# Expert weights by rows of sixteen kilobytes, a fourth split handed to GpSimd, and an earlier low half of the activations

## The chip, the core and the metric

The kernel runs on one core of one Trainium2 chip. The metric is the device time of one execution in microseconds. The kernel before takes 1289.53 us (median of three runs, 1288.2 to 1292.21). The execution that the profiler recorded took 1285.25 us; its span, from first to last instruction, is 1283.5 us.

## The reference

A decoder trunk with two residual layers on x of 512 tokens by 1024 features, float32. Each layer adds a mixer of the normed x (layer 0: gated recurrence beside differential attention; layer 1: gated linear attention), and then a mixture of experts:

```
h = rms_norm(x, ffn_norm)
per token: the best of 4 groups, the best 2 of its 4 experts, weights w
for e in 16 experts:
    act = silu(h @ w_gate[e]) * (h @ w_up[e])        # w_gate, w_up: 1024 x 512
    y  += combine[:, e] * (act @ w_down[e])          # w_down: 512 x 1024
x = x + y
```

A sum over the 1024 or 512 rows of a weight matrix may be taken in any order, if the rows of the weights and the columns of the other factor are ordered alike.

## The kernel before

Everything is written by engine, with semaphores written out by hand; no planner orders it. Float32 accuracy comes from splitting: a factor is rounded to a "high" part and the rest is the "low" part, and each product is three matmuls (high by high, high by low, low by high: `three`, L1106 to L1111).

Per layer, after the mixer, the second norm makes `h` (DVE, L1579), four tiles of 128 tokens. SyncE stores them as `h_rows` in DRAM. The router's scores are computed from x itself, DVE turns them into ranks and one-hots, and the first expert's rows are picked by matmul with a one-hot (L1343). Rows of the other experts are fetched by GpSimd with an indirect DMA of up to 96 rows (`gather`, L760 to L766), one expert at a time.

Then come the 16 experts, "blocks" 0 to 15 (`expert_loop`, L521; blocks 3 to 12 lie in a hardware loop of two blocks a turn). In block b:

- TensorE (`block_pe`, L1395): gate of expert b+1, with the four transposes of `act` of expert b in its middle (`act_T`, L1372, L1377); the eight transposes of the gathered rows of expert b+2 (`rows_T`, L1368); down of expert b; up of expert b+1. Gate, down and up are 24 matmuls of 512 columns each.
- ScalarE (`block_act`, L1028): the high part of the weights of down, in four pieces of 128x1024 (L870); the high part of `actT` (L1039); silu (L1024); the high part of up; the high part of the next rows (L1017); the high part of the next gate; the copy and store of y (L1060). Before each set of weights it waits until TensorE has finished the product before, since two sets share the buffers.
- VectorE (`block_ve`, L1872): the low part of the same weights, `low` (L1819, L1824: `expert_w - weight_high`, four pieces, each released by one piece of ScalarE's), for down, then the low part of `actT` (L1880), then `low` of up, the low part of the rows (L1832), `low` of gate, and `act = silu * up` (`times_up`, L1845). In block 1 it also computes slots (L1849), in block 13 the list of further blocks (`further`, L1858).
- SyncE (`block_loads`, L682) loads the next three weights of 2 MB (`load`, L649), each as soon as a product has freed its place. GpSimd only gathers (L801).

TensorE waits for a piece of low weights by a count on one semaphore (`wait_low`, L1357), and for the low part of `actT` before down (L1409, released by L1882). The last block's down weights ("LAST") are split apart from the others.

A weight matrix of 1024 rows lies in SBUF as 8 rows per partition; row k*128+p is in partition p. One partition's 8 rows (4 for down) are then 8 runs of 2 KB (4 of 4 KB) in DRAM.

Of the kernel before, what the change touches and what calls it, by code (L numbers as in the profile page):

```python
# [5 lines left out]
F32 = mybir.dt.float32  # L6
# [81 lines left out]
def build(nc, t):  # L88
# [149 lines left out]
    with ctx:  # L238
# [18 lines left out]
        def sem(name):  # L257
            return ctx.enter_context(nc.semaphore(name))
# [160 lines left out]
        oh0_ready = sem("first_onehot_ready")  # L419
        xgT_ready, ex_ready = sem("xgT_ready"), sem("gate_silu_ready")  # L420
        xgTh_ready, actTh_ready = sem("xgT_high_ready"), sem("actT_high_ready")
        w_hi, w_lo, w_lo_first = sem("weight_high_ready"), sem("weight_low_ready"), sem("first_low_ready")
        act_ready, actT_ready, y_ready, y_stored = sem("act_ready"), sem("actT_ready"), sem("y_ready"), sem("y_stored")
        yg_sem = [sem(f"y_gathered{i}") for i in range(2 * NT)]
# [128 lines left out]
        def high_count(l, pos, part):  # L553
            return SPLITS * (3 * NE * l + pos) + part + 1

        def low_count(l, pos, part):

            return SPLITS * ((3 * NE - 2) * l + pos - 2) + part + 1

        def parts(l, p0, par, part):  # L560

# [26 lines left out]
        def _(sp):  # L588
# [48 lines left out]
            for l in range(NL):  # L637
# [10 lines left out]

                def load(name, e, dst, done):  # L649

                    src = t["moe_w_" + name][l, bass.ds(e, 1)].rearrange("a (k p) n -> p (a k) n", p=P)
                    if name == "down":
                        dst = dst.rearrange("p (k c) n -> p k (c n)", c=2)
                    sp.dma_start(dst, src).then_inc(done, 16)
# [77 lines left out]
        def _(pool):  # L732
# [52 lines left out]
            for l in range(NL):  # L785
                for s in STEPS[l]:
                    if s == ("dT", 0, "dq", 0):
                        store_zeros()
                    if s[0] == "h":
                        power(xrs[:, s[2]:s[2] + 1])  # L790
                    elif s[0] == "sum":
                        power(dstd[:, s[3] % 2])
                    elif s[0] == "norm" or s[0] == "da" and s[2] >= 3 and (s[2] - 3) % NH == NH - 1:
                        power(rstd[:, 0:NH])

                pool.wait_ge(idx_ready, l + 1)
                pool.wait_ge(h_stored, 16 * NT * (l + 1))
                pool.sem_inc(gather_issued, 1)
                pool.indirect_dma_start(xg[0:CAP, :], None, hbuf[l][:], bass.IndirectOffsetOnAxis(idx[:, 1:2], 0)
                                        ).then_inc(gathered, 16)  # L800
                with pool.Fori(2, NE) as b:  # L801

                    bk.wait_full(pool, ("xgT", l), b - 1)
                    gather(l, b, idxcol_ready, b + (l * (NE - 2) - 1), gathered)
                pool.wait_ge(eid_ready, l + 1)
                more = pool.value_load(eid[0:1, 15:16], min_val=0, max_val=NX)
                pool.wait_ge(zero_stored, 16 * NL)
                with pool.If(more > 0):
                    pool.wait_ge(y_stored, 16 * (NE - 1) * (l + 1))
                    pool.wait_ge(ov_idx[l], 1)  # L810
                    with pool.Fori(0, NX) as b:
                        pool.wait_ge(ov_pe[l], b * 4 + 1)
                        gather(l, b + NE, ov_col[l], b + 1, ov_gathered[l])
                    pool.wait_ge(ov_act[l], 4 * NX)
                    gather_outputs(l, NB * CAP)
                with pool.If(more < 1):
                    pool.wait_ge(y_stored, 16 * (NE - 1) * (l + 1))
                    gather_outputs(l, NE * CAP)
# [283 lines left out]
        def _(pe):  # L1102
# [23 lines left out]
            for l in range(NL):  # L1126
# [230 lines left out]
                def wait_low(pos, b, part):  # L1357
                    if pos < 2:
                        pe.wait_ge(w_lo_first, SPLITS * (2 * l + pos) + part + 1)
                    else:  # L1360
                        pe.wait_ge(w_lo, b * (3 * SPLITS) + low_count(l, pos, part))

                def rows_T(b):
                    key = ("xgT", l)
# [107 lines left out]
        def _(ve):  # L1472
            link = Chain(ve, v_step)
            tt, ts, stt, cp = ve.tensor_tensor, ve.tensor_scalar, ve.scalar_tensor_tensor, ve.tensor_copy
            red = ve.tensor_reduce
            e_uses, n_st, roots = [0], [0], [0]

            def wait_e():
# [81 lines left out]
            for l in range(NL):  # L1560
# [7 lines left out]
                for s in STEPS[l]:  # L1568
                    kind = s[0]
                    if kind == "h":  # L1570
# [5 lines left out]
                                ve.wait_ge(h_stored, 16 * NT)  # L1576
                        ve.wait_ge(sq_done, NT * n + i + 1)
                        rsqrt(xrs[:, i:i + 1], xss[:, i:i + 1], D)
                        stt(h[:, i], x[:, i], xrs[:, i:i + 1], normw[:], ALU.mult, ALU.mult).then_inc(h_ready, 1)  # L1579
                    elif kind == "first" and s[2] == 0:  # L1580
                        first_low(0, range(SPLITS))
                        ve.wait_ge(rw_loaded, 16 * (NG + 4) * (l + 1))
# [254 lines left out]
                def times_up(b):  # L1837

                    ve.wait_ge(ex_ready, b + (l * NE + 1))

                    if l or not isinstance(b, int) or b:
                        s_, n_, _ = bk.uses[("actT", l)]
                        ve.wait_ge(bk.full[s_], b + (n_ - 1))
                    bk.wait_full(ve, ("up", l), b)
                    link(tt(act[0:CAP], bank(("up", l))[0:CAP], ex[0:CAP], ALU.mult))  # L1845
                    ve.sem_inc(act_ready, 1)
                    ve.sem_inc(bk.freed(("up", l)), 1)

# [23 lines left out]
                def block_ve(b, par):  # L1872

                    is_int = isinstance(b, int)
                    last = is_int and b == NE - 1
                    if not last:
                        low(DOWN, b, par)
                    key = ("actT", l)
                    ve.wait_ge(actTh_ready, b + (l * NE + 1))
                    link(tt(actTl[:].rearrange("p k n -> p (k n)"), bank(key)[:, 0:4 * CAP],  # L1880
                            actTh[:].rearrange("p k n -> p (k n)").bitcast(F32), ALU.subtract))
                    ve.sem_inc(actT_ready, 1)  # L1882
                    ve.sem_inc(bk.freed(key), 1)
                    if not last:
                        low(UP, b, par)
                    if not (is_int and b >= NE - 2):
                        rows_T(b + 2, par)
                        low(GATE + 3, b, par)
                    if is_int and b == NE - 2:
                        low(LAST, which=range(SPLITS - 1))  # L1890
                    if not last:
                        times_up(b + 1)
                    if is_int and b == NE - 2:
                        low(LAST, which=range(SPLITS - 1, SPLITS))
                    if is_int and b == 0:
                        slots()
                    if is_int and b == NE - 3:
                        further()
# [43 lines left out]
                with ve.If(more > 0):  # L1942
# [7 lines left out]
                    with ve.Fori(0, NX) as b:  # L1950
                        ve.wait_ge(ov_act[l], b * 4 + 2)
                        ve.wait_ge(ov_pe[l], b * 4 + 3)
                        tt(act[0:CAP], PS[0:CAP, 1, :], ex[0:CAP], ALU.mult).then_inc(ov_ve[l], 1)
            for kind, i in sums[NL - 1]:
                (add_gathered if kind == "x" else add_last)(NL - 1, i)

# [22 lines left out]
```

## Time and profile before

| | us |
|---|---|
| median of the runs | 1289.53 |
| the profiled execution | 1285.25 |
| its span | 1283.5 |
| TensorE busy | 1180.3 (92%) |
| VectorE busy | 914.7 (71%) |
| ScalarE busy | 674.1 (53%) |
| GpSimd busy | 97.3 (8%) |
| experts of layer 0, first to last matmul | about 361.6 to 661 |
| experts of layer 1 | about 966 to 1266 |

Busy times are of the profiled execution. A TensorE matmul is drawn with a length of 0.39 us although the next starts 0.23 us after it, so neighbours overlap, and short stops hide in the busy time; starts and named waits are the better reading. "PEld" is TensorE's weight load, "DVE" VectorE, "ACT" ScalarE, "POOL" GpSimd, "SP" SyncE. "DVEq L1882" as a releaser is the semaphore that VectorE's queue raises behind the instruction of L1880. Times of a timeline are counted from the span's start.

### The profile page before, as it was taken

The numbers are of one execution on the slowest core, as the hardware profiler recorded it, in microseconds if no ns is written. First come the engines' busy times: TensorE is split into PE (matmuls) and PEld (weight loads), VectorE is DVE, ScalarE is ACT, GpSimd is POOL, SyncE is SP. The second block draws the span as 40 slices with busy tenths as digits, with TensorE's granted clock in tenths as the row PEclk, the third lists the DMA queues.
The fourth block names the chain that finished last, engine by engine and source line by source line (L and its number), as shares of the span: only waits on it lengthen the run. The fifth ranks groups of instructions, "written<-read, shape, count | busy, mean of one in ns | idle before, by whom it ended". The sixth has DMA issues, their size and how long they took to land.

```text
span 1283.5 us, 16959 instructions
## 1 busy us (share of the span) xinstructions
PE 1180.3 (92%) x5788; PEld 898.5 (70%) x5788; DVE 914.7 (71%) x1251; ACT 674.1 (53%) x843; POOL 97.3 (8%) x128
## 2 busy tenths in 40 slices
PE   5999879999799999999878999999979999999986
PEld 4776669878776766766646688887876666667663
DVE  4646668656579888888967247646558898888886
ACT  4335651134347778777733242132426777787862
POOL 1120000000010000000030000001001100000003
PEclk9999999999899999999989999999979999999998
DMA  6231110123599999999860240113169999999955
GB/s 221 91 89 66 66 66 1 66 73 125 187 331 363 366 385 390 384 382 384 332 220 1 70 136 15 66 66 131 66 257 303 368 381 381 383 391 385 381 203 209
DMA packets 129423, 281.75 MB, mean 220 GB/s; under 512 B 18945, under 2 KB 19457, under 8 KB 129361
## 3 DMA queue, kind: packets, MB, share of 16 engines
q1 hardware_dynamic: 119680, 246.98, 53.2%
q0 software_dynamic: 5888, 20.97, 5.3%
q10 hardware_dynamic: 3792, 12.98, 2.7%
q8 instruction: 37, 0.61, 0.2%
q14 instruction: 26, 0.21, 0.1%
HBM read 262.05 MB, written 18.87 MB: 219 GB/s over the span
## 4 chain that ended last, share of the span: by engine, by line
PE 57%; DVE 25%; issue 9%; ACT 6%; POOL 1%; DMA 1%; DVEq 1%; ACTq 0%; SPq 0%
PE PS L1109 16%; PE PS L1111 15%; PE PS L1110 15%; DVE expert_w_low L1824 10%; PE PS L1213 4%; DVE group_low L1612 2%; PE PS L1343 2%; ACT weight_high L870 1%; PE PS L1148 1%; DVE xgT_low L1832 1%; DVE act L1845 1%; DVE score_max L1743 1%; DVE G L1502 1%; PE PS L1323 1%; DVE hT_low L1596 1%
## 5 line engine op out<-in xcount | busy, mean ns | idle before, releaser
L1824 DVE TENSOR_TENSOR expert_w_low<-expert_w,weight_high 128x1024 fp32r<-128x1024 f32 x368 | 426.5, 1221 | 75.0 <-ACT weight_high L870 71.3
L870 ACT ACTIVATE weight_high<-expert_w 128x1024 fp32r<-128x1024 f32 x384 | 375.5, 1049 | 69.6 <-PE PS L1111 61.9
L1109 PE MATMUL PS<-weight_high,xgT_high 128*96 128x512 f32 x512 | 204.5, 399 | 2.6 <-DVEq L1834 2.6
L1111 PE MATMUL PS<-weight_high,xgT_low 128*96 128x512 f32 x512 | 203.2, 397 | 0.0
L1110 PE MATMUL PS<-expert_w_low,xgT_high 128*96 128x512 f32 x512 | 202.1, 395 | 0.0
L1109 PE MATMUL PS<-group_high,hT_high 128*128 128x512 f32 x416 | 172.2, 414 | 13.9 <-DVEq L1599 9.5
L1111 PE MATMUL PS<-group_high,hT_low 128*128 128x512 f32 x416 | 165.3, 397 | 0.0
L1110 PE MATMUL PS<-group_low,hT_high 128*128 128x512 f32 x416 | 165.0, 397 | 0.0
L1109 PE MATMUL PS<-weight_high,actT_high 128*96 128x512 f32 x256 | 104.3, 407 | 19.4 <-DVEq L1882 18.9
L1612 DVE TENSOR_TENSOR group_low<-group_w,group_high 128x1024 fp32r<-128x1024 f32 x68 | 80.8, 1223 | 43.4 <-ACT group_high L894 39.5
L1109 PEld LDWEIGHTS PS<-weight_high,xgT_high 128*96 128x96 f32 x512 | 83.3, 163 | 36.0 <-DVEq L1834 2.7
L1111 PEld LDWEIGHTS PS<-weight_high,xgT_low 128*96 128x96 f32 x512 | 83.1, 162 | 36.1
L1110 PEld LDWEIGHTS PS<-expert_w_low,xgT_high 128*96 128x96 f32 x512 | 83.5, 163 | 34.5
L1111 PE MATMUL PS<-weight_high,actT_low 128*96 128x512 f32 x256 | 102.1, 399 | 0.0
L1109 PEld LDWEIGHTS PS<-group_high,hT_high 128*128 128x128 f32 x416 | 80.0, 192 | 31.1 <-DVEq L1599 10.9
L1110 PE MATMUL PS<-expert_w_low,actT_high 128*96 128x512 f32 x256 | 101.5, 396 | 0.0
L1111 PEld LDWEIGHTS PS<-group_high,hT_low 128*128 128x128 f32 x416 | 79.8, 192 | 18.0
L1110 PEld LDWEIGHTS PS<-group_low,hT_high 128*128 128x128 f32 x416 | 80.1, 193 | 15.0
L894 ACT ACTIVATE group_high<-group_w 128x1024 fp32r<-128x1024 f32 x68 | 69.7, 1057 | 27.3 <-PE PS L1111 21.7
L1213 PEld LDWEIGHTS PS<-Q,K 128*128 128x128 f32 x512 | 63.6, 199 | 12.4 <-DVEq L1669 6.5
L1213 PE MATMUL PS<-Q,K 128*128 128x64 f32 (+1 forms) x512 | 63.8, 280 | 8.1 <-DVEq L1669 5.7
L1109 PEld LDWEIGHTS PS<-weight_high,actT_high 128*96 128x96 f32 x256 | 41.8, 163 | 41.0 <-DVEq L1882 16.5
(251 smaller groups left out, 1469.9 us busy)
## 6 DMA issues: line engine op xcount, KB each, us to landing
expert_w<-in_moe_w_gate SPq DMA_DIRECT2D x32, 2048.0 KB, 13.7
expert_w<-in_moe_w_up SPq DMA_DIRECT2D x32, 2048.0 KB, 15.0
expert_w<-in_moe_w_down SPq DMA_DIRECT2D x32, 2048.0 KB, 13.5
group_w<-in_even_w_in SPq DMA_DIRECT2D x6, 2048.0 KB, 7.8
group_w<-in_odd_w_in SPq DMA_DIRECT2D x6, 2048.0 KB, 8.1
y_rows<-yb ACTq DMA_DIRECT2D x30, 384.0 KB, 6.1
group_w<-in_even_w_out SPq DMA_DIRECT2D x2, 2048.0 KB, 7.9
h_rows<-h SPq DMA_DIRECT2D x8, 512.0 KB, 11.3
```

The source lines that it names most:

```text
L870: act_(hi, w, ACT.Copy).then_inc(w_hi, 1)
L894: act_(hi, w, ACT.Copy).then_inc(g_hi_ready, 1)
L1109: pe.matmul(out, ah, bh, start=first, stop=False)
L1110: pe.matmul(out, ah, bl, start=False, stop=False)
L1111: return pe.matmul(out, al, bh, start=False, stop=final)
L1148: ins = pe.transpose(bank(k)[:, c * P:(c + 1) * P], src[:, i, d:d + P], ident[:])
L1213: ins = pe.matmul(out, K[:, c, cols], q, start=True, stop=True)
L1323: ins = pe.matmul(bank(key)[:, i * NR:(i + 1) * NR], xT[:, k, i * P:(i + 1) * P], rw[:, k, :], start=k == 0, stop=k == KD - 1)
L1343: ins = pe.matmul(PS[:, 4 + c // 4, c % 4 * CAP:(c % 4 + 1) * CAP], h[:, i, c * P:(c + 1) * P], oh0[:, i], start=i == 0, stop=i == NT - 1)
L1502: ins = stt(dst[:, c * dv:(c + 1) * dv], z[:, c * dv:(c + 1) * dv], rstd[:, c:c + 1], outer(c), ALU.mult, ALU.mult)
L1612: tt(lo, w, hi.bitcast(F32), ALU.subtract).then_inc(g_lo_ready, 1)
L1824: tt(lo, w, hi.bitcast(F32), ALU.subtract).then_inc(w_lo, 1)
```

## The change

Three things.

1. `block_ve`: the low part of `actT` is computed after three of the four pieces of down, not after all four. The fourth piece of down follows it.
2. The fourth piece of `low` of up leaves VectorE and goes to GpSimd, in blocks 0 to 14 of each layer (30 instructions in all), with a semaphore of its own; the counts of the other are adapted. GpSimd's gathers are written in pairs, with one `up_low` behind each but the first.
3. Expert weights are loaded so that partition p holds rows 8p to 8p+7 (4p to 4p+3 for down): one run of 16 KB for each partition. To match, `h` of the second norm and `act` are stored with their columns in the order k, j instead of j, k. VectorE writes them without a stride and reads its operands with one: 8 elements for x and the norm weight (8 instructions of 128x1024 in all), 4 elements for `act`'s two inputs (32 of 96x512). The transposes, the stores and the gathers are unchanged.

```diff
+        LOWS = 3 * SPLITS - 1
+
         def low_count(l, pos, part):
 
-            return SPLITS * ((3 * NE - 2) * l + pos - 2) + part + 1
+            done = SPLITS * (pos - 2) - (pos - 2) // 3
+            return (SPLITS * (3 * NE - 2) - (NE - 1)) * l + done + part + 1
...
-                    src = t["moe_w_" + name][l, bass.ds(e, 1)].rearrange("a (k p) n -> p (a k) n", p=P)
+                    src = t["moe_w_" + name][l, bass.ds(e, 1)].rearrange("a (p k) n -> p (a k) n", p=P)
...
-                with pool.Fori(2, NE) as b:
+                def next_rows(b):
 
                     bk.wait_full(pool, ("xgT", l), b - 1)
                     gather(l, b, idxcol_ready, b + (l * (NE - 2) - 1), gathered)
+
+                def up_low(b, par):
+
+                    w, hi, lo = parts(l, UP, par, SPLITS - 1)
+                    pool.wait_ge(w_hi, b * (3 * SPLITS) + high_count(l, UP, SPLITS - 1))
+                    pool.tensor_tensor(lo, w, hi.bitcast(F32), ALU.subtract).then_inc(w_lo_pool, 1)
+
+                next_rows(2)
+                next_rows(3)
+                up_low(0, 0)
+                with pool.Fori(0, (NE - 4) // 2) as k:
+                    next_rows(k * 2 + 4)
+                    up_low(k * 2 + 1, 1)
+                    next_rows(k * 2 + 5)
+                    up_low(k * 2 + 2, 0)
+                up_low(NE - 3, 1)
+                up_low(NE - 2, 0)
...
-                        pe.wait_ge(w_lo, b * (3 * SPLITS) + low_count(l, pos, part))
+                        if pos == UP and part == SPLITS - 1:
+                            pe.wait_ge(w_lo_pool, b + (l * (NE - 1) + 1))
+                        else:
+                            pe.wait_ge(w_lo, b * LOWS + low_count(l, pos, part))
...
+            act_parts = act[0:CAP].rearrange("p (k j) -> p k j", k=DE // P)
+
+            def in_parts_of(a):
+                return a.rearrange("p (j k) -> p k j", k=DE // P)
...
-                        stt(h[:, i], x[:, i], xrs[:, i:i + 1], normw[:], ALU.mult, ALU.mult).then_inc(h_ready, 1)
+                        dst, xi, nw = h[:, i], x[:, i], normw[:]
+                        if n % 2:
+
+                            dst = dst.rearrange("p (k j) -> p k j", k=KD)
+                            xi, nw = (a.rearrange("p (j k) -> p k j", k=KD) for a in (xi, nw))
+                        stt(dst, xi, xrs[:, i:i + 1], nw, ALU.mult, ALU.mult).then_inc(h_ready, 1)
...
-                    link(tt(act[0:CAP], bank(("up", l))[0:CAP], ex[0:CAP], ALU.mult))
+                    link(tt(act_parts, in_parts_of(bank(("up", l))[0:CAP]), in_parts_of(ex[0:CAP]), ALU.mult))
...
                     if not last:
-                        low(DOWN, b, par)
+                        low(DOWN, b, par, range(SPLITS - 1))
                     key = ("actT", l)
                     ve.wait_ge(actTh_ready, b + (l * NE + 1))
                     link(tt(actTl[:].rearrange("p k n -> p (k n)"), bank(key)[:, 0:4 * CAP],
@@
                     ve.sem_inc(bk.freed(key), 1)
                     if not last:
-                        low(UP, b, par)
+                        low(DOWN, b, par, range(SPLITS - 1, SPLITS))
+                        low(UP, b, par, range(SPLITS - 1))
```

(`act` of the overflow path, L1953, which these inputs don't enter, is changed in the same way.)

## Rows read from the trace of the kernel before

**Rows 1.** Busy time by stretch: experts of layer 0; then clock, DMA share, GB/s.
```profile
420.00:600.00 180.00, 177.40 (x832) 125.23 (x831) 157.20 (x149) 142.46 (x160) 11.12 (x20) 1.00 1.04 382
```

**Rows 2.** TensorE's waits (us in total, times, longest) in 356:420, 403:632, 610:665.
```profile
PE PS L1109 <- DVEq L1882: 2.3, 2, 1.6
...
PE PS L1109 <- DVEq L1882: 2.6, 5, 0.6
...
PE PS L1109 <- DVEq L1882: 4.6, 2, 3.2
```

**Rows 3.** TensorE's timeline: start, length; first matmul of down in blocks 6, 7, 14.
```profile
492.28 0.47 PE L1109 MATMUL PS<-weight_high,actT_high 128*96 128x512 f32 x1
...
510.76 0.46 PE L1109 MATMUL PS<-weight_high,actT_high 128*96 128x512 f32 x1 [0.58 <-DVEq L1882]
...
639.74 0.47 PE L1109 MATMUL PS<-weight_high,actT_high 128*96 128x512 f32 x1 [3.22 <-DVEq L1882]
```

**Rows 4.** VectorE's timeline: up of block 6 to actT_low of block 7.
```profile
493.66 4.63 DVE L1824 TENSOR_TENSOR expert_w_low<-expert_w,weight_high 128x1024 fp32r<-128x1024 f32 x4 [1.57 <-ACT weight_high L870]
498.21 0.95 DVE L1832 TENSOR_TENSOR xgT_low<-PS,xgT_high 128x768 fp32r<-128x768 f32 x1
499.48 4.63 DVE L1824 TENSOR_TENSOR expert_w_low<-expert_w,weight_high 128x1024 fp32r<-128x1024 f32 x4 [0.32 <-DVE xgT_low L1832]
504.03 0.68 DVE L1845 TENSOR_TENSOR act<-PS,ex 96x512 f32<-96x512 f32 x1
505.47 4.63 DVE L1824 TENSOR_TENSOR expert_w_low<-expert_w,weight_high 128x1024 fp32r<-128x1024 f32 x4 [0.77 <-ACT weight_high L870]
510.02 0.55 DVE L1880 TENSOR_TENSOR actT_low<-PS,actT_high 128x384 fp32r<-128x384 f32 x1
```

**Rows 5.** ScalarE's timeline: high parts of up (block 6) and of the next gate.
```profile
492.56 3.91 ACT L870 ACTIVATE weight_high<-expert_w 128x1024 fp32r<-128x1024 f32 x4 [0.18 <-ACT ex L1024]
...
498.10 3.91 ACT L870 ACTIVATE weight_high<-expert_w 128x1024 fp32r<-128x1024 f32 x4 [0.93 <-PE PS L1111]
```

**Rows 6.** Groups by line and shape, VectorE: busy us, mean ns.
```profile
L1782 DVE TENSOR_TENSOR r_dif<-r_ge 128x320 f32<-128x320 f32 x2 | 1.4, 721 | 0.1
...
L1781 DVE TENSOR_TENSOR r_ge<-r_ge,earlier 128x320 f32<-128x320 f32 x2 | 1.0, 491 | 0.1
```

**Rows 7.** Groups by line and shape, GpSimd.
```profile
L774 POOL TENSOR_TENSOR da_rstd<-da_rstd,minus_half 128x8 f32<-128x8 f32 x8 | 13.1, 1642 | 62.2 <-DVE da_rstd L1648 62.2
...
L741 POOL TENSOR_SCALAR_AFFINE_SELECT tri_before<-ones 128x128 f32<-128x128 f32 x1 | 0.3, 283 | 0.0
```

**Rows 8.** GpSimd's timeline: the gather in block 6, and the first gather.
```profile
493.48 0.93 POOL L765 DMA_INDIRECT xg<-h_rows,idxcol  x1 [0.80 <-POOL idxcol L762]
...
362.32 1.41 POOL L799 DMA_INDIRECT xg<-h_rows,idx  x1 [22.66 <-DVEq L1918]
```

**Rows 9.** VectorE's timeline: last tile of the norm, start of the routing (layer 0).
```profile
339.69 1.28 DVE L1579 SCALAR_TENSOR_TENSOR h<-x_sb,x_rstd,norm_weight 128x1024 f32<-128x1024 f32 x1 [0.67 <-POOL x_rstd L774]
340.89 0.23 DVE L1770 TENSOR_TENSOR r_L<-PS,x_rstd 128x80 f32<-128x80 f32 x1
```

**Rows 10.** VectorE's timeline: `act` of block 15, layer 0.
```profile
653.20 0.68 DVE L1845 TENSOR_TENSOR act<-PS,ex 96x512 f32<-96x512 f32 x1
```

**Rows 11.** The page: DMA queues (packets, MB, share) and issues (median us to landing).
```profile
q1 hardware_dynamic: 119680, 246.98, 53.2%
...
q8 instruction: 37, 0.61, 0.2%
...
expert_w<-in_moe_w_up SPq DMA_DIRECT2D x32, 2048.0 KB, 15.0
...
xg<-h_rows,idxcol POOLq DMA_INDIRECT x28, 7.2
```

**Rows 12.** SyncE's timeline: the load of expert 8's up weights.
```profile
485.97 0.37 SPq L654 DMA_DIRECT2D expert_w<-in_moe_w_up  x1
```

**Rows 13.** TensorE's timeline: transposes of expert 1's rows, in block 0's up.
```profile
371.35 0.82 PE L1368 MATMUL PS<-ident,xg 96*128 96x96 f32 x8
```

More of the change, by code:

```diff
@@ L421, in build @@
         xgTh_ready, actTh_ready = sem("xgT_high_ready"), sem("actT_high_ready")
+        w_lo_pool = sem("weight_low_by_gpsimd_ready")
         w_hi, w_lo, w_lo_first = sem("weight_high_ready"), sem("weight_low_ready"), sem("first_low_ready")
@@ L1952, in _ @@
                         ve.wait_ge(ov_pe[l], b * 4 + 3)
-                        tt(act[0:CAP], PS[0:CAP, 1, :], ex[0:CAP], ALU.mult).then_inc(ov_ve[l], 1)
+                        tt(act_parts, in_parts_of(PS[0:CAP, 1, :]), in_parts_of(ex[0:CAP]), ALU.mult).then_inc(ov_ve[l], 1)
             for kind, i in sums[NL - 1]:
```

## Prediction

> **What bounds the kernel now.** I read the busy times by stretch first, then TensorE's waits, then the timelines of one pair of blocks. In 420 to 600 us, ten of layer 0's blocks, TensorE is busy for 177.40 of 180 us, VectorE for 157.20, and the DMA engines show a full share at 382 GB/s [rows 1]. So TensorE is the bound, VectorE has some 13% to spare, and the queues look full. What ends last is seen in the waits: TensorE stands still only at the first matmul of down, and always for VectorE's semaphore behind the low part of `actT` (L1882). Layer 0 loses 2.3 us to it in the first blocks, 2.6 us in five later ones, 4.6 us in the last two [rows 2]: 9.5 us, and layer 1, which repeats the pattern, about as much. No wait names a DMA.
>
> A pair of blocks shows why. Down starts at 492.28 without a wait and at 510.76 with one of 0.58 [rows 3], so TensorE's own block takes 510.76 - 492.28 - 0.58 = 17.90 us. In the late one, `act` ends at 504.71, four pieces of low for down run from 505.47 to 510.1, `actT_low` ends at 510.57, and TensorE starts 0.19 later [rows 4]. The four pieces stand ahead of `actT_low` without need: TensorE wants the first of them together with it, but the fourth only at its 19th matmul.
>
> **Part 1, `actT_low` ahead of the fourth piece.** One piece is 4.63 / 4 = 1.16 us [rows 4]. `actT_low` comes 1.16 us sooner, which is more than the 0.58 of the pairs. The fourth piece then ends about 0.5 us later than before, some 3.5 us ahead of its matmuls. It costs nothing.
>
> **Part 2, the fourth piece of up on GpSimd.** VectorE has 1.16 us less a block. But that doesn't shorten the late chain: VectorE's next pieces (499.48) wait for ScalarE's first high part of the next gate (498.10 and 1.1 us, so 499.2), and that waits for TensorE [rows 5]. So this is room, not time. What matters is what GpSimd costs. The trace has no two-operand subtraction of 1024 elements there. From below: a one-input select of 128 elements takes 0.283 us [rows 7]; eight times that is an upper reading of the same cost at 1024, 2.3 us, and with a fixed part of 0.1 us taken off each time 1.5 us. From above: the power of 8 elements takes 1.64 us, 0.2 us an element, 210 us for 1024; that operation is another kind of work, so I go by the select and take 2.3 us, bounds 1.5 and twice 2.3 (two operands), 4.6. Its last high part is there at 492.56 + 3.91 = 496.5 [rows 5], its gather was issued by 494.4 [rows 8], and TensorE starts up at about 497.9 and needs the fourth piece 18 matmuls of 0.23 us later, at 502.1. So even 4.6 us would be in time, as far as GpSimd alone is concerned, and the next gather is a block away.
>
> The trace has no GpSimd instruction of any length beside VectorE's pieces. If the two got in each other's way, VectorE's piece of 499.2 would move. It may start at 499.4 at the latest: 510.18 (TensorE ready) less 0.19, `actT_low` 0.5, three pieces 3.5, the gap of 0.76 behind `act`, `act` 1.2 (part 3) and its own four pieces 4.6. In every second block that gap is smaller (down isn't late there), say 0.4, which gives 499.8. VectorE's three pieces of up end at 493.66 + 3.5 = 497.15, and the low part of the rows, one operand of which is in PSUM, lies between. A GpSimd piece held back until 497.15 that then holds VectorE back until it ends is harmless up to 2.3 us in the one kind of block and 2.7 us in the other. The Trainium skill states such a rule (SBUF — State Buffer, "Who interferes with whom"): a VectorE instruction with both inputs in SBUF and a GpSimd instruction that reads SBUF exclude each other for the whole instruction. By its GPSIMD Engine Reference, "Elementwise — side-by-side cycle accounting", 4497 ns for 2048 elements, such a piece would be about 2.3 us (an estimate), and the rule would then just cost nothing here; no row shows either.
>
> **Part 3, strides on VectorE.** The one row with an operand read at a step of 4 elements is L1782: 721 ns for 320 elements, against 491 for the same size without it [rows 6]. Its rows are four elements long, so three steps of four are strided: 230 ns / 240 = 0.96 ns for each, one more cycle. `act` then costs 0.68 + 512 x 0.96 = 0.49, 1.17 us; I use +0.5. A tile of the norm, two operands at a step of 8, costs 1.28 + 1.0 = 2.3 us. Bounds: nothing (two rows are all there is), and twice that, if both operands pay.
>
> Where it falls: of the four norm tiles of a layer only the last stands straight in front of the routing [rows 9], with TensorE idle behind it: +1.0 us a layer. The other three lie beside matmuls. `act` is in VectorE's chain ahead of down, so it eats 0.5 of part 1's 1.16 wherever VectorE leads, and in block 15 it is added whole: there `act` (653.20) follows pieces of LAST, whose order isn't changed [rows 10].
>
> **Part 4, runs of 16 KB.** The load of expert 8's up is issued at 485.97 [rows 12] and lands about 15.0 us later [rows 11], at 501.0; ScalarE takes it a block after 492.56, at 510.4. Nine us of slack: faster loads bring nothing. Queue q1 needs 0.532 x 16 x 1283.5 us / 119680 = 91 ns for a packet of about 2 KB, 361 GB/s over 16 engines. The only packets of 16 KB, q8's instruction fetches, need 0.002 x 16 x 1283.5 / 37 = 1.1 us, 240 GB/s [rows 11]; those go elsewhere, and I don't take that rate, but it is the other end. The Trainium skill (DMA: Bandwidth & Descriptors, "Why small descriptors are slow (HBM only)") has a fixed overhead per packet, so longer ones gain a few per cent; by the trace this would only land loads earlier. The tightest fetch is the first gather: issued at 362.32 [rows 8], 7.2 us to landing [rows 11], used at 371.35 [rows 13], 1.8 us of slack.
>
> **The sum, per layer.** Blocks 0 and 1: down(0) gains 1.16 - 0.5 = 0.6, down(1) again 0.6, 1.2 of their 2.3. The five waits of the pairs: 2.6, all. Block 14 (3.22 of wait, behind `further`): 0.6. Block 15: -0.5. Norm: -1.0. Together 2.9 us, and 5.8 for two layers. On the profiled execution's own time 1285.25 - 5.8 = 1279.5; that execution lies 4.3 us under the median, so against the runs shown 1289.5 - 5.8 = 1283.7 us. What is late next is TensorE itself, at 17.9 us a block.
>
> **The rivals.** (a) The strides cost nothing. Then blocks 1, 14, 15 gain 0.5 each, block 0 0.1 (it is down to TensorE), the norm 1.0: 2.7 a layer, 11.2 in all, 1278.3 us. For it: only one row shows a penalty. Against: that row is the same step of 4. (b) GpSimd's piece holds VectorE up, or is slowed by it. Place: `low` of the next gate, in some 12 blocks a layer; price: its length over 2.3 us in half of them, over 2.7 us in the others. It decides from 12 x (d - 2.3) + 12 x (d - 2.7) = 5.8, d = 2.75 us; at 3.5 us it costs 14.4 + 9.6 = 24, so 1307.7 us. For it: by my value there is nothing to spare in half of the blocks, and the select has one operand where this has two. Against: VectorE stands idle at that place anyway, waiting for ScalarE. (c) The strides cost more. At one and a half times my price `act` is up 0.75 and the norm 1.5: blocks 0, 1 and 14 gain 0.4 each, the pairs (0.76 of gap kept) 0.37 each, block 15 loses 0.75, together 0.8 a layer, 1287.9 us. At twice: 0.15 each, 0.12 each, -1.0, -2.0, so -1.95 a layer and 1293.4 us. A gather of expert 1 that long packets delay beyond its 1.8 us of slack would add to it. (d) Packets of 16 KB at q8's rate: 6.3 MB an expert would take 26 us instead of 17.9, 1550 us. Nothing but that row speaks for it.
>
> **Numbers.** Forecast 0.45, (a) 0.15, (b) 0.19, (c) 0.17, (d) 0.04. About 0.3% (3.9 us) is what a measurement tells from no change. Three quarters of the forecast's mass and all of (a) lie beyond it: faster 0.49. The rest of the forecast, two thirds of (c) and a little of (b): same 0.26. Slower 0.25. Range 1276.5 to 1296: it takes in (a), (c) and the beginning of (b).
>
> **What would show it.** In the changed kernel the waits for `actT_low` in the pairs are gone and down starts every 17.9 us; VectorE's `act` lasts about 1.2 us and the odd norm tiles 2.3; GpSimd has 30 pieces of about 2.3 us, which end before 500 in the block shown here; landings are no later than 15 us. It is wrong if TensorE still waits at down or at the fourth piece of up, if VectorE's pieces begin behind GpSimd's ends, if `act` is far from 1.2, or if a DMA appears as a releaser in the expert blocks.

## The result, and the profile after

The changed kernel takes 1270.95 us (median of three runs, 1270.85 to 1276.44) against 1289.53 before: ratio 0.9866, 95% interval 0.9819 to 0.9913. By the profiled executions it is 1285.25 - 1270.95 = 14.3 us faster; the forecast was 5.8. Run again beside the experiments, the same kernel took 1276.32 us (1273.46 to 1277.6) against 1287.45: ratio 0.9907, interval 0.989 to 0.9924. The two comparisons overlap. What moves inside them is TensorE's granted clock: the run of 1276.44 had a mean of 0.966, those of 1270.95 and 1270.85 had 0.973 and 0.971. The two profiled executions of the same kernel differ in span by 5.5 us (1269.0 and 1274.5), and their stretches at the lower clock level, 1.2 GHz, sum to 71 and 85 us, beside 85 in the kernel before. I take 0.9907, 11 to 12 us, as the change's size, and put the first result's surplus down to the clock.

TensorE in the stretch of [rows 1], kernel after: start and end, length, then busy us of TensorE's matmuls and weight loads, VectorE, ScalarE, GpSimd, then granted clock, DMA share, GB/s.

```profile
420.00:600.00 180.00, 180.00 (x855) 128.05 (x854) 157.59 (x143) 145.50 (x164) 53.44 (x32) 1.00 1.01 394
```

TensorE has no idle time left there (177.40 before). VectorE's busy time didn't fall, although it has a twelfth fewer pieces of low to do (338 instead of 368 in the whole run). The reason is seen below: some of its pieces last longer beside GpSimd's.

TensorE's timeline after, first matmuls of down in blocks 6, 7, 14, with the transposes of rows ahead of two of them (start, length, in brackets the idle time before and its releaser), which answer to [rows 3]:

```profile
488.29 0.82 PE L1392 MATMUL PS<-ident,xg 96*128 96x96 f32 x8
488.89 0.45 PE L1130 MATMUL PS<-weight_high,actT_high 128*96 128x512 f32 x1
...
505.95 0.82 PE L1392 MATMUL PS<-ident,xg 96*128 96x96 f32 x8
506.62 0.47 PE L1130 MATMUL PS<-weight_high,actT_high 128*96 128x512 f32 x1
...
632.60 0.47 PE L1130 MATMUL PS<-weight_high,actT_high 128*96 128x512 f32 x1 [2.64 <-DVEq L1916]
```

The transposes of block 6 before, which stand ahead of the 492.28 of [rows 3]:

```profile
491.51 0.82 PE L1368 MATMUL PS<-ident,xg 96*128 96x96 f32 x8
```

And those of block 7 before, ahead of the 510.76 with its printed wait of 0.58:

```profile
509.36 0.82 PE L1368 MATMUL PS<-ident,xg 96*128 96x96 f32 x8
```

These are the rows that I should have read. The first matmul of down follows the first of the transposes by 0.77 us in block 6 and by 1.40 us in block 7. After, it is 0.60 in block 6 and 0.67 in block 7, and in the kernel with the order alone (below) it is 0.60 to 0.61 in every block from 2 to 13: that is the distance of a start that nothing holds. So before, down is held by about 0.17 us in block 6, where no wait is printed, and by 0.8 us in block 7, where 0.58 is printed. The printed wait is counted from the drawn end of the transposes (509.36 + 0.82 = 510.18), and an unheld down starts 0.2 us ahead of that end. VectorE's line for `actT_low` of block 6 before, which the prediction didn't look at, says what holds block 6:

```profile
491.54 0.55 DVE L1880 TENSOR_TENSOR actT_low<-PS,actT_high 128x384 fp32r<-128x384 f32 x1
```

It ends at 492.09, and down starts 0.19 us later, the very distance by which it follows `actT_low` in block 7, where a wait is printed. Summed in this way over blocks 2 to 13 of layer 0, the starts of down are held by 4.9 us before, of which 2.6 are printed, and by 0.5 us after. After the change, block 7 starts 506.62 - 488.89 = 17.73 us behind block 6, and the blocks of the stretch stand 17.67 to 17.77 apart.

VectorE's timeline after, block 6 into block 7, for [rows 4]:

```profile
487.65 0.55 DVE L1914 TENSOR_TENSOR actT_low<-PS,actT_high 128x384 fp32r<-128x384 f32 x1
...
490.43 3.50 DVE L1858 TENSOR_TENSOR expert_w_low<-expert_w,weight_high 128x1024 fp32r<-128x1024 f32 x3 [0.69 <-ACT weight_high L891]
...
495.79 4.91 DVE L1858 TENSOR_TENSOR expert_w_low<-expert_w,weight_high 128x1024 fp32r<-128x1024 f32 x4 [0.86 <-ACT weight_high L891]
500.62 1.08 DVE L1879 TENSOR_TENSOR act<-PS,ex 96x512 f32<-96x512 f32 x1
502.46 3.50 DVE L1858 TENSOR_TENSOR expert_w_low<-expert_w,weight_high 128x1024 fp32r<-128x1024 f32 x3 [0.77 <-DVE act L1879]
505.88 0.55 DVE L1914 TENSOR_TENSOR actT_low<-PS,actT_high 128x384 fp32r<-128x384 f32 x1
```

GpSimd's piece beside them:

```profile
493.32 2.89 POOL L814 TENSOR_TENSOR expert_w_low<-expert_w,weight_high 128x1024 fp32r<-128x1024 f32 x1 [0.86 <-ACT weight_high L891]
```

`act` takes 1.08 us (0.68 before). GpSimd's piece is shown from 493.32 to 496.21, but until 493.93 VectorE's own pieces run, and VectorE's next four take 4.91 us in place of 4.63. Where VectorE has no gap, in block 14, its four down and up pieces beside GpSimd's (2.56 us, from 634.75) show what that means:

```profile
632.72 6.81 DVE L1858 TENSOR_TENSOR expert_w_low<-expert_w,weight_high 128x1024 fp32r<-128x1024 f32 x4 [0.24 <-DVE actT_low L1914]
```

They take 6.81 us where four take 4.63: the 2.2 us of GpSimd's piece are added whole. The same is seen in block 1, where VectorE computes the slots too and has no gap either:

```profile
400.19 6.84 DVE L1858 TENSOR_TENSOR expert_w_low<-expert_w,weight_high 128x1024 fp32r<-128x1024 f32 x4 [0.25 <-DVE actT_low L1914]
```

There it isn't free: down of block 2 comes 18.03 us behind block 1 (18.37 in layer 1), where it is 17.68 in the kernel without GpSimd's piece.

The time by stretch, between first matmuls of down (us; before, after, difference, forecast):

```
start to block 0, layer 0         382.67  381.27  -1.40  +0.4
block 0 to block 14, layer 0      257.07  251.33  -5.74  -3.8
block 14 to 15, layer 0            16.19   16.54  +0.35  +0.5
block 15 to block 0 of layer 1    330.84  329.36  -1.48  +0.4
block 0 to block 14, layer 1      257.32  251.45  -5.87  -3.8
block 14 to 15, layer 1            16.19   16.53  +0.34  +0.5
block 15 to the end                23.22   22.52  -0.70   0
sum (the spans' difference)                       -14.50  -5.8
```

The -1.40 is seen in the stretch where block 0's gate begins (windows of before, then of after; columns as above):

```profile
361.50:364.50 3.00, 2.91 (x7) 2.04 (x8) 2.92 (x3) 0.00 (x0) 1.41 (x1) 0.50 1.02 360
```

```profile
361.50:364.50 3.00, 2.82 (x12) 2.02 (x13) 2.83 (x3) 0.00 (x0) 1.40 (x1) 1.00 1.00 421
```

TensorE starts gate at 361.59 before and 361.68 after, yet before it has the lower clock level, 1.2 GHz, for 3.4 us (7 matmuls in 3 us in place of 12). This isn't the change's doing in every run. In the repeated run of the changed kernel the two stretches that end in a block 0 are 1.1 and 0.9 us longer than before, not 1.4 and 1.5 shorter, while block 0 to block 14 is 5.8 and 5.9 us shorter there too. Only the latter two I count as the change's.

DMA, the rows that answer to [rows 11]:

```profile
q1 hardware_dynamic: 50048, 246.98, 51.1%
...
expert_w<-in_moe_w_up SPq DMA_DIRECT2D x32, 2048.0 KB, 12.1
```

There are fewer packets, up lands 2.9 us sooner, the stores of y land later (8.7 us after issue, 6.1 before), and no wait of TensorE in the expert blocks names a DMA.

### The profile page after: what moved, and what is told of

Read it like the earlier page. It is cut to its first block, busy times and chain, and to the rows that moved or that the text cites. A ratio compares the mean times of both kernels' runs of the same rounds, so it can differ in the third digit from the quotient of the medians.

```text
span 1269.0 us, 16898 instructions
## 1 busy us (share of the span) xinstructions
PE 1169.8 (92%) x5788; PEld 894.1 (70%) x5788; DVE 918.4 (72%) x1221; ACT 673.3 (53%) x843; POOL 208.7 (16%) x158
## 4 chain that ended last, share of the span: by engine, by line
PE 68%; DVE 21%; ACT 4%; issue 3%; DMA 1%; POOL 1%; DVEq 0%; ACTq 0%; POOLq 0%; SPq 0%
PE PS L1130 19%; PE PS L1132 19%; PE PS L1131 18%; DVE expert_w_low L1858 6%; PE PS L1234 4%; DVE group_low L1646 2%; PE PS L1364 1%; PE PS L1169 1%; PE PS L1392 1%; DVE score_max L1777 1%; DVE h L1613 1%; DVE x_sb L1585 1%; DVE G L1531 1%; PE PS L1344 1%; DVE hT_low L1630 1%
## 5 line engine op out<-in xcount | busy, mean ns | idle before, releaser
L1858 DVE TENSOR_TENSOR expert_w_low<-expert_w,weight_high 128x1024 fp32r<-128x1024 f32 x338 | 408.7, 1262 | 63.6 <-ACT weight_high L891 40.9
L814 POOL TENSOR_TENSOR expert_w_low<-expert_w,weight_high 128x1024 fp32r<-128x1024 f32 x30 | 86.3, 2877 | 86.6 <-ACT weight_high L891 86.6
L1132 PEld LDWEIGHTS PS<-group_high,hT_low 128*128 128x128 f32 x416 | 79.7, 192 | 17.9
L778 POOL TENSOR_TENSOR rstd<-rstd,minus_half 128x4 f32<-128x4 f32 x12 | 12.1, 1009 | 375.1 <-DVE rstd L1514 375.1
```

The costliest lines, as they stand in the source:

```text
L814: pool.tensor_tensor(lo, w, hi.bitcast(F32), ALU.subtract).then_inc(w_lo_pool, 1)
L1132: return pe.matmul(out, al, bh, start=False, stop=final)
L1858: tt(lo, w, hi.bitcast(F32), ALU.subtract).then_inc(w_lo, 1)
```

## The experiments

The kernels ran in groups of four, each group on one chip with runs of the kernel before beside it (medians 1287.45, 1286.54 and 1288.18 us); the ratios are to those, so kernels of different groups are compared by ratio.

### The order alone, and its combinations

Edit of the order alone (the other three add or leave out the other parts of the diff whole):

```diff
-                        low(DOWN, b, par)
+                        low(DOWN, b, par, range(SPLITS - 1))
 ...
                     if not last:
+                        low(DOWN, b, par, range(SPLITS - 1, SPLITS))
                         low(UP, b, par)
```

> Before with only the order changed: the low half of act is issued ahead of the fourth down piece; all up pieces stay on VectorE, loads stay in 2 KB runs, no strides. Theory A (the gain came from the held starts of the down matmuls, the unmarked ones of some 0.2 us in the even blocks included): the down starts of blocks 1 to 13 stand 17.68 us apart as in after, b0 to b13 about 230 us, the layer 5 to 6 us shorter, 1274 us beside 1285 (ratio 0.991). Rival B (the order is worth only its marked waits, VectorE needs the relief by GpSimd for the rest): pairs of blocks stay near 35.6 us, 2 to 3 us a layer, 1280 us (0.996). Rival C (the 16 KB runs made the matmuls' stream faster): spacing stays at 17.90, about 1281 to 1283.

Measured: 1269.55 us (1267.98 to 1270.65), ratio 0.9855 [0.9836, 0.9875]. The down starts of blocks 1 to 13 stand 17.66 to 17.69 us apart in both layers; block 0 to 14 takes 250.24 us, 6.8 and 7.1 less than before. Theory A's structure holds to the hundredth, but its gain was too small: 11 us expected, 18 measured. B and C fall. What theory A didn't have is in block 14:

```profile
634.41 0.47 PE L1109 MATMUL PS<-weight_high,actT_high 128*96 128x512 f32 x1 [2.35 <-DVEq L1882]
```

and the 4.5 us behind it (windows):

```profile
634.50:639.00 4.50, 4.50 (x20) 3.17 (x21) 4.46 (x4) 2.28 (x3) 0.00 (x0) 1.00 1.05 400
```

In before and after a stretch at 1.2 GHz follows at this place, and block 15 comes 16.19 and 16.54 us behind block 14; here 14.62. Over the whole run, though, this kernel has 85 us at 1.2 GHz, as many as before: other stretches are longer, behind block 15 among them. So what the missing stretch is worth in the whole time isn't shown; the spans differ by 14.6 us, the stretches from block 0 to 15 by 17.

Order and GpSimd's piece:

> Order and GpSimd's up piece, without the 16 KB runs and the strides. Theory A: within 1 us of the order alone, as VectorE has idle time in each pair of blocks in either; in block 14 the last low pieces come 1 to 2 us sooner than in the order alone. Rival B: 3 us a layer faster than the order alone. If the strides cost what they show (act 0.39 us a block, the norm tile 0.8 us) and the 16 KB runs give nothing, this one is the fastest of the four, by 1 to 3 us under after.

Measured: 1270.4 us (1265.37 to 1272.86), 0.9855 [0.9832, 0.9877]. There is no difference from the order alone, and it lies 5.9 us under the changed kernel, where 1 to 3 were expected. Block 14 is held 2.24 us instead of 2.35. B falls again.

Everything but GpSimd's piece:

> After without GpSimd's piece: order, 16 KB runs and strides, all up pieces on VectorE. Theory A: spacing of the down starts 17.68 or little more (17.7 to 17.8), within 2 us of after. Rival B: marked waits of 0.5 us and more in each second block, as the act is 0.39 us longer and VectorE 4 us a pair more loaded: 1277 to 1280.

Measured: 1276.98 us (1273.64 to 1278.19), 0.9909 [0.9892, 0.9927], equal to after. The spacings are 17.67, with four of 17.9 to 18.0 in each layer, so less even than theory A had it, and far from rival B's waits of 0.5 us. So the piece buys 0.2 to 0.3 us in four blocks, where the longer `act` has used the room up, loses 0.35 and 0.7 us of it in block 2, and brings nothing that the time shows.

The change again, on the same chip:

> The changed kernel again, on the chip of the other three, so that they can be compared: 1271 us, 0.986 of before by either theory; if it is 0.990 or above, a part of the first difference was the chip's and not the kernel's.

Measured: 1276.32 us, 0.9907 [0.989, 0.9924]. By what was written ahead, 0.990 or above means that a part of the first difference wasn't the kernel's. It is 7 us over the order alone: the rest of the change costs more than a third of what its first part brings.

### Runs or strides

After without the strides:

```diff
-    stt(dst, xi, xrs[:, i:i + 1], nw, ALU.mult, ALU.mult)
+    stt(h[:, i], x[:, i], xrs[:, i:i + 1], normw[:], ALU.mult, ALU.mult)
 ...
-    link(tt(act_parts, in_parts_of(bank(("up", l))[0:CAP]), in_parts_of(ex[0:CAP]), ALU.mult))
+    link(tt(act[0:CAP], bank(("up", l))[0:CAP], ex[0:CAP], ALU.mult))
```

> After without the strided reads of norms and act (the 16 KB runs stay, so columns are multiplied with other rows of the weights; this part of the computation is changed). Theory S (the 16 KB runs are worth nothing, the strides cost the 6 us by which after stands above the kernel with order and GpSimd's piece alone): about 1270 us, 0.9855 of before, block 14 held 2.2 to 2.3 us, no half clock there. Rival R (the long packets cost it: gathered rows land 11.6 us after issue instead of 8, stored rows 8.9 instead of 6): stays at 1276, 0.991. Rival G (the runs gain, the strides cost more than 6): under 1268.

This kernel leaves out the reordering of the columns of `h` and `act`, so they are multiplied with other rows of the weights. It runs as many instructions as the changed kernel. The next three leave out a part of the reordering, or have it without the long runs; they too compute something else, with as many instructions as the kernel before.

Measured: 1264.68 us (1264.16 to 1268.97), 0.9848 [0.9826, 0.9871]; block 14 held 2.24, no half clock there, 14.62 us to block 15. By ratio it can't be told from the order with GpSimd's piece, which has 2 KB runs (0.9855): theory S. R falls. G isn't ruled out by the time: 1264.68 is under its 1268, but on this chip the kernel before is faster as well, and by ratio it comes to 1268. A gain by the long runs isn't shown.

The order with the strides and the short runs:

> Before with the new order and the strided reads, but loads in 2 KB runs (columns are multiplied with other rows, this part of the computation is changed). Theory S: 1276 to 1277 us as with the 16 KB runs (0.991), block 14 held 2.75 us and a stretch at half clock behind it. Rival R: about 1270 (0.9855), as the order alone.

Measured: 1277.28 us (1273.04 to 1279.78), 0.993 [0.9909, 0.9952]. Theory S. Block 14 and the window behind it:

```profile
635.00 0.47 PE L1109 MATMUL PS<-weight_high,actT_high 128*96 128x512 f32 x1 [2.76 <-DVEq L1892]
```

```profile
635.00:639.50 4.50, 4.50 (x13) 3.04 (x14) 4.37 (x4) 1.96 (x3) 0.00 (x0) 0.62 1.05 400
```

13 matmuls where the order alone has 20. Block 0 to 14 takes 1.7 and 1.9 us more than in the order alone, block 14 to 15 another 1.9 (0.4 for `act`, 1.5 for the clock at this place).

### Which stride

Only `act` with the stride, on top of the order:

> The new order with act written with the stride (and the norm plain), 2 KB runs (columns are multiplied with other rows, this part of the computation is changed). Of the 7.7 us by which order and both strides stand above the order alone, theory A puts most here: 0.4 us at each of blocks 0, 1, 14, 15, 0.25 in each of 4 blocks more, and 1.5 us of half clock behind the longer wait in block 14, per layer 4 us, so 1276 us (0.992). Rival (the norm tiles cost it, 0.9 us each on the path to routing): under 1272 (0.988).

Measured: 1278.04 us (1274.21 to 1280.5), 0.9934 [0.9914, 0.9953]: as slow as with both strides (0.993). `act` takes 1074 ns in the mean, and the spacings are those of both strides (251.92 us from block 0 to 14, then 16.54).

Only the norm:

> The new order with the norm of the expert blocks written with the stride (and act plain), 2 KB runs (columns are multiplied with other rows, this part of the computation is changed). Theory A: block spacings as in the order alone (17.67), block 14 held 2.35 us, first down start at most 0.5 us a layer later: 1270 us (0.987). Rival: each of the four tiles' 0.8 us stands on the path, up to 3 us a layer: 1276.

Measured: 1269.68 us (1268.46 to 1273.05), 0.9876 [0.9854, 0.9897]. The spacings are those of the order alone, 14.62 us from block 14 to 15. Against the order alone the time is 0.1 us more by the medians and 2.7 by the ratios, whose intervals overlap; the rival of 3 us a layer falls. The strided tiles do cost something ahead of the blocks. In layer 0 the gate of block 0 begins 22.2 to 22.3 us behind the start of the last norm tile in the five kernels with the strides in the norm, and 21.8 to 21.9 in the nine without: 0.4 us.

### GpSimd alone and GpSimd doubled

Before with GpSimd's piece and nothing else:

> Before with GpSimd's fourth up piece alone: old order (four down pieces ahead of actT_low), 2 KB runs, no strides. Theory A (the down matmuls are held by the chain act, four down pieces, actT_low, which the relief doesn't shorten): the held starts stay, 17.86 to 18.5 apart, 0.71, 1.6 and 3 us at blocks 0, 1 and 14: within 2 us of before, ratio 0.998 to 1.002. Rival (VectorE's load sets the pairs): the marked waits of the odd blocks (0.58) go, 3 us a layer, 0.995; the unmarked 0.18 stays.

Measured: 1285.94 us (1283.22 to 1289.66), 0.9994 [0.9982, 1.0006]. The waits of blocks 0, 1 and 14 are the old ones (0.71, 1.64, 3.21); those of the pairs shrink from 0.58 to 0.38 and 0.43 (about 0.25 in layer 1) but don't go. Block 0 to 14 takes 1.1 and 1.3 us less than before, and block 14 to 15 takes 1.1 and 1.2 us more, with 6.8 us at 1.2 GHz at that place. So VectorE's load has a small part in the pairs; the limit is the place of `actT_low`.

Two of the four up pieces on GpSimd, with the new order:

```diff
-    w, hi, lo = parts(l, UP, par, SPLITS - 1)
-    pool.wait_ge(w_hi, b * (3 * SPLITS) + high_count(l, UP, SPLITS - 1))
-    pool.tensor_tensor(lo, w, hi.bitcast(F32), ALU.subtract).then_inc(w_lo_pool, 1)
+    for part in (SPLITS - 2, SPLITS - 1):
+        w, hi, lo = parts(l, UP, par, part)
+        pool.wait_ge(w_hi, b * (3 * SPLITS) + high_count(l, UP, part))
+        pool.tensor_tensor(lo, w, hi.bitcast(F32), ALU.subtract).then_inc(w_lo_pool, 1)
```

> The new order, no layout change, with the third and the fourth up piece on GpSimd, two pieces of 2.9 us a block in place of one. Theory A with the exclusion of the two engines: GpSimd's second piece ends at about 8.7 us behind the down start where the single one ends at 7.3, VectorE's four gate pieces, which start 6.9 behind it now and may start 0.5 to 0.9 later at no cost, are late by 0.9 to 1.8 us: down starts 18.3 to 19 us apart, 16 to 30 us more than with one piece, ratio 1.00 to 1.01. Rival (GpSimd costs VectorE nothing that counts): 17.67 apart, ratio 0.9855, as with one.

Measured: 1285.79 us (1284.02 to 1289.66), 0.9991 [0.9979, 1.0002]. The whole gain is gone. GpSimd, VectorE and TensorE in blocks 6 and 7:

```profile
496.17 4.95 POOL L815 TENSOR_TENSOR expert_w_low<-expert_w,weight_high 128x1024 fp32r<-128x1024 f32 x2
```

```profile
499.62 5.99 DVE L1854 TENSOR_TENSOR expert_w_low<-expert_w,weight_high 128x1024 fp32r<-128x1024 f32 x4 [1.01 <-ACT weight_high L892]
```

```profile
511.13 0.47 PE L1131 MATMUL PS<-weight_high,actT_high 128*96 128x512 f32 x1 [0.52 <-DVEq L1912]
```

VectorE's four gate pieces take 5.99 us (4.91 beside one GpSimd piece, 4.63 beside none), and down, which hangs on them through `act` and `actT_low`, waits 0.52 us. Pairs take 17.8 + 18.4 = 36.2 us instead of 35.3. Theory A's mechanism holds; its spacings of 18.3 and more were too high, and the ratio lies at the lower edge of what it gave.

### A better order

The list of further blocks moved:

```diff
                     if is_int and b == NE - 2:
+                        further()
                         low(LAST, which=range(SPLITS - 1))
 ...
-                    if is_int and b == NE - 3:
-                        further()
```

> The order alone, and the seven instructions that make the list of further blocks (2.8 us of VectorE at the end of block 13) moved to block 14, where VectorE stands 2.6 us idle ahead of the last block's low pieces. Theory A: the 2.35 us ahead of the down matmuls of block 14 is gone in both layers, block 14 starts 17.67 after block 13, and block 15 gives back at most 0.3: 4 to 4.7 us less than the order alone, 1265 us (0.982). Rival: SyncE's loads for the next layer wait for that list and come 10 us later, the next layer starts later: 1268 to 1272. Rival 2: the wait in block 14 only moves to block 15, as the high pieces of the last block set it: 1269.

Measured: 1266.17 us (1265.54 to 1270.18), 0.9849 [0.9829, 0.987]. The wait of block 14 is gone (no bracket in either layer, 17.06 us behind block 13), but the transposes of `act` of block 15 now wait 2.4 us instead of 1.3: 1.55 us a layer remain by the down starts, 3.1 in all where 4 to 4.7 were expected. The second rival has part of it. Down of block 0 of layer 1 comes 333.0 us behind block 15, 1.2 us later than in the order alone. The first rival would have such a delay; the clock (3 us more at 1.2 GHz between the two) would explain it as well, and no run separates them. By the ratio the whole is 0.0006 of the time, which can't be told from nothing.

And the last block's pieces in smaller portions:

```diff
-    low(LAST, which=range(SPLITS - 1))
+    low(LAST, which=range(SPLITS - 2))
 ...
-    low(LAST, which=range(SPLITS - 1, SPLITS))
+    low(LAST, which=range(SPLITS - 2, SPLITS - 1))
 ...    # behind actT_low
+    if last:
+        low(LAST, which=range(SPLITS - 1, SPLITS))
```

> As the last, and the four low pieces of the last block's down weights are put as 2, act, 1, actT_low, 1 instead of 3, act, 1, actT_low. Theory: act of block 15 comes up to 1.16 us sooner, the 1.34 us ahead of its transposes falls to 0.2 to 0.5: 1 us a layer less than the last, 1263 us. Rival: the pieces wait for ScalarE's high pieces anyway, no change against the last.

Measured: 1266.45 us (1261.83 to 1269.35), 0.9845 [0.982, 0.9869]. The wait ahead of the transposes is back at 1.2, not at the 0.2 to 0.5 expected, yet block 13 to 15 takes 31.50 us: 1.1 us less than the last, as expected, and 2.7 us a layer less than the order alone (34.19). By time it can't be told from the last or from the order alone; its trace has the shortest span. It beats the kernel before and, by its ratio, the change as run again (0.9907).

## Why the prediction was wrong

**What bounds the kernel**: right. TensorE, held only at down by `actT_low`.

**TensorE's own block, 17.90 us**: the step that failed, and with it the term of 2.6 us a layer for the pairs. It took the printed waits for all that TensorE was held, in two ways. From 510.76 - 492.28 = 18.48 it took off the printed 0.58, but that start was held by 0.8 us, so the block is 17.67 us. And it took 492.28, a start without a bracket, for a start without a wait, though it was held by 0.17 us. From block 1 to block 13 the traces give 217.09 - 212.68 = 4.4 us in layer 0 and 4.5 in layer 1, in place of 2.6. Rows of before held the answer: the distances 0.77 and 1.40 us behind the transposes, and the 0.19 us behind `actT_low`, alike in both blocks.

**Part 1**: the mechanism is right, its size not. Without the strides, my numbers give 1.1 + 2.6 + 1.1 = 4.8 us a layer from block 0 to 14; alone it brings 6.8 and 7.1, and 1.6 more behind block 14, where the shorter wait goes with a TensorE at 2.4 GHz. That second term wasn't in my sum. The change as made has it in one of the four layers profiled, since the longer `act` brings the wait of block 14 back from 2.24 to 2.64 us.

**Part 2**: "room, not time" is right (0.9994 alone, no difference on top of the order). The price, 2.3 us, came out as 2.89 in the trace, of which 0.6 is waiting behind VectorE's pieces: 2.3 net. The exclusion that the Trainium skill states (SBUF — State Buffer, "Who interferes with whom") is what this case's traces show: 6.81 us for 4.63 in block 14. The deadline worked out for it was right for the blocks that it was worked out for: VectorE's gate pieces get 0.28 us longer and nobody waits. Block 2 wasn't looked at, and there down is late by 0.35 and 0.7 us. Rival (b) is a true mechanism that costs no more than this here; with two pieces it decides.

**Part 3**: `act` +0.4 for the forecast +0.5. (The sum printed there has a slip: 512 x 0.96 ns is 0.49 us, and 0.68 + 0.49 is 1.17. Another is in rival (a): its terms add up to 2.6 a layer, not 2.7, so 1278.5 us.) The odd norm tiles take 2.17 us in the mean ((2 x 1728) - 1284 ns), 2.09 for the last one of layer 0, where I had 2.3. But of the +1.0 a layer for the norm only 0.4 is there: counted from the start of the last norm tile (339.69 before, 339.37 after), the gate of block 0 begins 21.90 us later before and 22.31 after. Why the other 0.4 us of the longer tile is made up wasn't followed. Block 14 to 15, +0.5 forecast, is +0.35.

**Part 4**: right that they bring nothing: with and without the long runs the time is the same (0.9848, 0.9855). That they land weights sooner isn't clear from the runs. Between these two kernels up lands in 14.9 instead of 15.8 us, gate in 14.6 instead of 13.8, down in 14.7 in both; and the kernel with GpSimd's piece doubled lands up in 12.2 with short runs. The fetch that I had called the tightest is: in the repeated run of the change the first gather of layer 0 landed at 373.11, 8.8 us after its issue, and TensorE, idle for 1.1 us, began its transposes at 373.20.

**The sum**: block 0 to 14 gave 2.0 us a layer more than forecast, 4.0 in all, in the first run and in the repeated one. Of the rest of the first run's surplus, 3.7 us lie in the two stretches that end in a block 0, and that part is luck: in the repeated run, whose time at 1.2 GHz is that of before (85 us), they hold nothing of it, and the spans differ by 1283.5 - 1274.5 = 9.0 us.

**The rivals**: (a) is nearest in time, 1278.3, but not in cause: the strides do cost, 6 to 8 us in the two comparisons with GpSimd's piece and 8 to 10 in the one without it, and nearly all of it by `act`. (c) and (d) fell by the trace. That the order alone would beat the change wasn't among them.

## What to carry to other kernels

A start without a printed wait isn't proof of an engine that runs free, and a printed wait isn't all that it was held. Take the distance to the end of what it needs, and compare it with that distance where a wait is shown: if they are equal, it is held. Then take the distance from the engine's own instruction before it, here 0.61 us when free and 1.40 where 0.58 was printed: the difference is the true hold, and the floor is lower than the spacing less the printed wait. A change of several parts can hold its gain in one and its cost in another: here 18 us came from moving one instruction ahead of another, and 7 us went to a longer instruction on the chain that the first had just freed.

## What the runs showed of the hardware

A printed wait of TensorE before block 14's down of 2.63 us or more had a stretch at 1.2 GHz with it or behind it in 15 of 16 layers of the profiled kernels, one of 2.23 to 2.36 us in none of 8. Where the stretch came, 0.4 us of VectorE went with 1.5 us more behind the wait. That the longer wait brought the stretch is a reading of these counts; no run varies the wait alone. Reading PSUM and SBUF at a step of 4 elements costs `act` 0.39 us for 512 elements, 0.77 ns each; a norm tile at a step of 8 costs 0.89 us for 1024, 0.87 ns each. A VectorE piece and a GpSimd piece that both read two operands from SBUF take their turns: four of the one and one of the other take 6.81 us, 4.63 + 2.2. In the four kernels with weights in 16 KB runs the gathered rows of the later experts land 11.3 to 11.6 us after issue (median), in the others 7.2 to 8.1, and nothing waited for them here. The first gather of a layer, which TensorE did wait for in two executions (1.1 us with long runs, 0.3 with short ones), shows no such difference: 5.5 to 8.8 against 6.3 to 8.0 us.
